# A two-block transformer on one core: first loads split, weights split earlier, retention's heads and PEER's end in another order

## The reference

```
# first block, for l in 0, 1
x = x + 0.5 * swiglu(rms_norm(x, ffn1_norm[l]), gate, up, down)        # 1024 -> 2816 -> 1024
h = rms_norm(x, mix_norm[l]); a, g, q, k, v = split(h @ w_in[l])
x = x + concat([conv_module(a, g), diff_attention(q, k, v)]) @ w_out[l]
x = x + 0.5 * swiglu(rms_norm(x, ffn2_norm[l]), gate, up, down)
# second block, for layer in 0, 1
mod = silu(c) @ ada_w[layer] + ada_b[layer]         # shifts, scales and gates
x = x + g1 * mixer(modulate(rmsnorm(x), sh1, sc1))  # layer 0: retention (4 heads), layer 1: sgu
x = x + g2 * peer_ffn(modulate(rmsnorm(x), sh2, sc2))
# at the end
return rmsnorm(x, norm_final)
```

## Time and profile before

| what | value |
| --- | --- |
| median of three runs | 3076.28 us |
| the three runs | 3084.94, 3076.28, 3075.04 us |
| the profiled execution's own time | 3079.91 us |
| its span in the profile | 3078.1 us |
| PE busy | 3023.9 us, 98% |
| DVE busy | 2184.3 us, 71% |
| ACT busy | 1611.1 us, 52% |
| POOL busy | 266.6 us, 9% |
| from HBM | 616.55 MB |

### The profile page before, as it was taken

One profiled execution on the slowest core, in us unless ns is written; L12 is line 12 of the kernel. 1 busy time (PEld: TensorE's weight loads), 2 busy tenths in 40 slices (PEclk: granted clock), 3 DMA queues, 4 the chain that ended last, 5 costly groups with the idle time before them and its releaser, 6 DMA issues.

```text
span 3078.1 us, 53282 instructions
## 1 busy us (share of the span) xinstructions
PE 3023.9 (98%) x22540; PEld 2851.7 (93%) x22540; DVE 2184.3 (71%) x3454; ACT 1611.1 (52%) x2390; POOL 266.6 (9%) x249
## 2 busy tenths in 40 slices
PE   8999999999999999999999999999999999999999
PEld 8998999999899998999999998879999999999887
DVE  5877887876788746899555557675669975555676
ACT  5575544565544455556544445556445554444444
POOL 0010001000101001830000000000156000000000
PEclk9999999999999999999999999999999999999999
DMA  6772577775267544457866657655444687666663
GB/s 230 268 250 96 205 252 253 266 268 194 97 248 282 179 154 172 157 179 286 290 218 218 215 201 244 210 182 187 165 168 175 233 298 238 218 218 218 220 232 123
DMA packets 153260, 654.59 MB, mean 213 GB/s; under 512 B 10332, under 2 KB 77472, under 8 KB 78272
## 3 DMA queue, kind: packets, MB, share of 16 engines
q1 hardware_dynamic: 96576, 584.09, 53.3%
q10 hardware_dynamic: 56032, 65.66, 6.4%
q0 software_dynamic: 416, 1.45, 0.2%
HBM read 616.55 MB, written 34.61 MB: 212 GB/s over the span
## 4 chain that ended last, share of the span: by engine, by line
PE 88%; DVE 8%; ACT 2%; issue 1%; DMA 1%; POOL 0%; ACTq 0%; DVEq 0%
PE ps L596 19%; PE ps L598 19%; PE ps L597 19%; PE ps L601 8%; PE ps L602 8%; PE ps L603 8%; DVE w_lo L1544 2%; PE ps L1025 2%; PE ps L764 2%; ACT w_hi L1094 1%; DVE raw L1539 0%; DVE h_lo L1562 0%; PE ps L996 0%; DVE at L2034 0%; DVE at L2024 0%
## 5 line engine op out<-in xcount | busy, mean ns | idle before, releaser
L1544 DVE TENSOR_TENSOR w_lo<-raw,w_hi 128x1024 fp32r<-128x1024 f32 x932 | 1137.7, 1227 | 597.8 <-ACT w_hi L1094 596.7
L1094 ACT ACTIVATE w_hi<-raw 128x1024 fp32r<-128x1024 f32 x1000 | 1050.6, 1055 | 679.7 <-PE ps L598 429.2
L596 PE MATMUL ps<-h_hi,w_hi 128*128 128x256 f32 x4224 | 1186.2, 281 | 7.3 <-DVE w_lo L1544 6.1
L597 PE MATMUL ps<-h_lo,w_hi 128*128 128x256 f32 x4224 | 1177.0, 279 | 0.0
L598 PE MATMUL ps<-h_hi,w_lo 128*128 128x256 f32 x4224 | 1176.8, 279 | 0.0
L596 PEld LDWEIGHTS ps<-h_hi,w_hi 128*128 128x128 f32 x4224 | 794.1, 188 | 13.5 <-issue 6.2
L598 PEld LDWEIGHTS ps<-h_hi,w_lo 128*128 128x128 f32 x4224 | 799.9, 189 | 0.0
L597 PEld LDWEIGHTS ps<-h_lo,w_hi 128*128 128x128 f32 x4224 | 795.0, 188 | 2.8 <-issue 0.2
L601 PE MATMUL ps<-w_hi,at 128*128 128x512 f32 x1024 | 398.5, 389 | 3.1 <-DVE at L2083 3.1
L602 PE MATMUL ps<-w_lo,at 128*128 128x512 f32 x1024 | 398.3, 389 | 0.0
L603 PE MATMUL ps<-w_hi,at 128*128 128x512 f32 x1024 | 398.3, 389 | 0.0
(11 more groups left out here) (281 smaller groups left out, 3259.1 us busy)
## 6 DMA issues: line engine op xcount, KB each, us to landing
raw<-in_peer_u SPq DMA_DIRECT2D x128, 1024.0 KB, 4.8
raw<-in_peer_v SPq DMA_DIRECT2D x128, 1024.0 KB, 4.8
raw<-in_ffn_gu SPq DMA_DIRECT2D x88, 1024.0 KB, 4.9
raw<-in_ada_w SPq DMA_DIRECT2D x48, 1024.0 KB, 5.2
raw<-in_ffn_down SPq DMA_DIRECT2D x44, 1024.0 KB, 4.9
gates<-at ACTq DMA_DIRECT2D x32, 1024.0 KB, 4.6
at<-gates ACTq DMA_DIRECT2D x24, 1024.0 KB, 5.9
raw<-in_w_in SPq DMA_DIRECT2D x16, 1024.0 KB, 4.8
```

The source lines that it names most:

```text
L596: e.matmul(o, lhs[0], rhs[0], start=start, stop=False)
L597: e.matmul(o, lhs[0], rhs[1], start=False, stop=False)
L1094: e.activation(whi[:, u % NPAIR, :], raw(k, half), ACT.Copy).then_inc(hi_done.hit(u), 1)
L1544: e.tensor_tensor(wlo[:, m % NPAIR, :], raw(k, half), whi[:, m % NPAIR, :].bitcast(FP), ALU.subtract).then_inc(w_lo_dve.hit(m), 1)
```

## The change

It does the following.

1. **First loads.** x is loaded in two halves (ACT's queue, with the columns of gains between them), the first raw tile in two halves (SP's queue, `raw_first`). The second raw tile waits for x's first half, the third for its second. ACT splits unit 0, then all of h, then unit 1; before it was unit 0, 1, then h. PE no longer waits for `ident`, `half` and x at its start, and its first pair is two `project` calls in turn in place of the interleaved pair. `lam` moves behind the first four splits.
2. **First FFN.** ACT splits units 8 and 9 ahead of `rr`, the silu table and silu of c; before they came among the first silu steps. DVE does the same.
3. **Mixer's output.** Each of ACT and DVE splits one unit more before it waits for x and h there, ACT does its two `h_split` before its two `square`, and `NSUM` of q = 2 and 5 falls from 6 to 4: POOL adds four squares, ACT makes four, and PE sums two of these inside the next FFN's first pair (`inside`).
4. **Adaptive weights.** 17 of each 80 tiles are skipped in place of 14, and the rest stand closer (48 per 122 positions in place of 128).
5. **Retention.** Three banks for scores, gates and sums, four for `attend`. PE does `attend` after pairs 1, 2, 4, 5 and `finish` after 2, 3, 5, 6. DVE inverts a head's root at once and finishes that head a pair later (`invert`, `split`). Nothing stands between pair 7 and `ret_out` on PE. 
6. **PEER's end.** The last pair of `peer_v` runs accumulators 0 and 1 for both units before 2 and 3. ACT copies three accumulators, DVE the last. ACT's squares have five buffers (`square_tile`) for q = 8 and 10.

```diff
-NSUM = {1: 7, 2: 6, 3: 7, 4: 7, 5: 6, 6: 7, 7: 7, 9: 7}
+NSUM = {1: 7, 2: 4, 3: 7, 4: 7, 5: 4, 6: 7, 7: 7, 9: 7}
...
-        seen += not 33 <= i % 80 < 47
-        while n_ada < 48 and n_ada < (seen - 2) * 48 // 128:
+        seen += not 33 <= i % 80 < 50
+        while n_ada < 48 and n_ada < (seen - 2) * 48 // 122:
...
+        ATTEND, FINISH = {1: 0, 2: 1, 4: 2, 5: 3}, {2: 0, 3: 1, 5: 2, 6: 3}
...
+            def project_pairs(q, key, n, outs, lag=2, inside=None):
                 for at in range(KT + lag * (len(outs) - 1)):
+                    if at == inside:
+                        added_sums(q)
+                        sums(q, at, at)
+                        sums(q, at + 1, at + 1)
...
                     if f == 0:
-                        project_pairs(q, (f"{which}_gu", l), 0, [b])
-                        if c > 0:
+                        if c == 0:
+                            for half in range(2):
+                                project(q, unit[(f"{which}_gu", l), half], b[:, half * T:(half + 1) * T])
+                        else:
+                            project_pairs(q, (f"{which}_gu", l), 0, [b], inside=NSUM[q] if NSUM[q] < KT - 2 else None)
+                        if c == 2:
                             added_sums(q)
-                        for m in (0, 1) if c == 0 else range(NSUM[q], KT):
+                        for m in (0, 1) if c == 0 else range(max(NSUM[q], KT - 2), KT):
                             sums(q, m, m)
...
# PE, retention
-                    if n % 2 == 1:
-                        attend(n // 2)
-                    if n % 2 == 0 and n >= 2:
-                        finish(n // 2 - 1)
-                finish(3)
+                    if n in FINISH:
+                        finish(FINISH[n])
+                    if n in ATTEND:
+                        attend(ATTEND[n])
...
# PE, peer
-                    for e2 in range(2):
+                    for e2, ks in ((0, range(4)), (1, range(4))) if n < 63 else ((0, (0, 1)), (1, (0, 1)), (0, (2, 3)), (1, (2, 3))):
...
-                        for k in range(4):
+                        for k in ks:
...
-                        t.then_inc(used.hit(g), 1)
+                        if ks[-1] == 3:
+                            t.then_inc(used.hit(g), 1)
...
# ACT, ffn and mixer
-                token_scale(q, unit[(f"{which}_gu", l), 1] + 1 + NPAIR if c > 0 else 0)
+                ahead = 1 if c > 0 else 5
+                token_scale(q, unit[(f"{which}_gu", l), ahead] + 1 + NPAIR)
...
+                w_hi_upto(unit[("w_out", l), 4] + NPAIR)
                 for n in range(4):
-                    w_hi_upto(unit[("w_out", l), 4 + n] + NPAIR)
+                    if n < 3:
+                        w_hi_upto(unit[("w_out", l), 4 + n] + 1 + NPAIR)
                     w.wait_ge(x_upd, x_upd(q + 1, 2 * n + 1))
                     for m in (2 * n, 2 * n + 1):
                         h_split(q + 1, m, gains)
+                    for m in (2 * n, 2 * n + 1):
                         if m >= NSUM[q + 1]:
                             square(q + 1, m, m)
...
# ACT, peer's end
-                for k in range(2):
+                for k in range(3):
                     w.wait_ge(acc_done, acc_done(l, k))
-                    e.activation(orow[:, k, 0:512], acc[k], ACT.Copy).then_inc(orow_a.hit(l, k), 1)
+                    e.activation(orow[:, k % 2, k // 2 * 512:k // 2 * 512 + 512], acc[k], ACT.Copy).then_inc(orow_a.hit(l, k), 1)
...
# ACT, start
-            e.dma_start(x, a["x"]).then_inc(loads["x"].sem, 16)
+            e.dma_start(x[:, 0:4], a["x"][:, 0:4]).then_inc(loads["x"].sem, 16)
             e.dma_start(cols, a["cols"]).then_inc(loads["cols"].sem, 16)
+            e.dma_start(x[:, 4:8], a["x"][:, 4:8]).then_inc(loads["x2"].sem, 16)
...
-            w_hi_upto(2)
+            w_hi_upto(1)
             w.wait_ge(loads["cols"], 16)
-            w.wait_ge(loads["x"], 16)
             for m in range(KT):
+                w.wait_ge(loads["x" if m < 4 else "x2"], 16)
                 h_split(0, m, col("ffn1_norm", 0))
+            w_hi_upto(2)
...
# DVE, mixer's output
+                w_lo_upto(unit[("w_out", l), 4] + NPAIR)
                 for n in range(4):
-                    if n < 3:
-                        w_lo_upto(unit[("w_out", l), 4 + n] + NPAIR)
                     w.wait_ge(*unit_after(("w_out", l), 4 + n))
...
+                    if n < 3:
+                        w_lo_upto(unit[("w_out", l), 4 + n] + 1 + NPAIR)
                     for m in (2 * n, 2 * n + 1):
                         h_split(q + 1, m, gains)
...
# DVE, retention
-                    if n % 2 == 0 and n >= 2:
-                        finish(n // 2 - 1)
+                    if n in (3, 4, 6):
+                        finish((3, 4, 6).index(n))
+                    if n in FINISH:
+                        invert(FINISH[n])
                 finish(3)
...
# SP, start
-                if 0 < k < NRAW:
-                    w.wait_ge(loads["x"], 16)
+                if k == 0:
+                    e.dma_start(raw_t[:, 0, 0:UNIT], src[:, 0:UNIT]).then_inc(raw_first.sem, 16)
+                    e.dma_start(raw_t[:, 0, UNIT:2 * UNIT], src[:, UNIT:2 * UNIT]).then_inc(landed[0].sem, 16)
+                    continue
+                if k < NRAW:
+                    w.wait_ge(loads["x" if k == 1 else "x2"], 16)
```

More of the change, by code:

```diff
@@ L266, in build @@
         banks = Banks([0, 1, 2, 3, 4, 5])
-        loads = {n: signal(f"load_{n}") for n in ("x", "cols", "ident", "half", "c", "iota", "relb", "oh", "anti")}
+        loads = {n: signal(f"load_{n}") for n in ("x", "x2", "cols", "ident", "half", "c", "iota", "relb", "oh", "anti")}
         consts = signal("consts_set", lambda n: n + 1)
@@ L675, in scale_row @@
                 w.wait_ge(rc_inv, rc_inv(q))
+                w.wait_ge(loads["ident"], 16)
                 for tt in range(2):
@@ L771, in qk_sums @@
                     w.wait_ge(qk_sq, qk_sq(l, i))
+                    w.wait_ge(loads["half"], 16)
                     for tt in range(2):
@@ L895, in retention @@
                     project_rows(q, "ret_v", c, 2 + c, ("rv", c))
+                wide = Banks([banks.ids[(banks.at + d) % 6] for d in (1, 2, 3, 4)])
+                narrow = Banks([banks.ids[(banks.at + d) % 6] for d in (5, 6)] + [6])
                 def scores(hh):
-                    b = take(banks, ("rsc", hh))
+                    b = take(narrow, ("rsc", hh))
                     w.wait_ge(rq_rot, rq_rot(2 * hh + 1))
@@ L909, in attend @@
                     for e2 in range(2):
-                        b = take(banks, ("ratt", hh, e2))
+                        b = take(wide, ("ratt", hh, e2))
                         for z in range(2):
@@ L917, in finish @@
                 def finish(hh):
-                    b = take(banks, ("rfin", hh))
+                    b = take(narrow, ("rfin", hh))
                     for z in range(4):
@@ L924, in retention @@
                 for n in range(8):
-                    b = take(banks, ("rg", n))
+                    b = take(narrow, ("rg", n))
                     project(q, unit["ret_g", 2 * n], b[:, 0:T])
@@ L1068, in _ @@
             w.wait_ge(consts, 1)
-            w.wait_ge(loads["ident"], 16)
-            w.wait_ge(loads["half"], 16)
-            w.wait_ge(loads["x"], 16)
             for l in range(L):
@@ L1506, in _ @@
             e.activation(rcol, epsc, ACT.Sqrt)
+            w_hi_upto(1)
+            w.wait_ge(loads["cols"], 16)
+            for m in range(KT):
+                w.wait_ge(loads["x" if m < 4 else "x2"], 16)
+                h_split(0, m, col("ffn1_norm", 0))
             w_hi_upto(2)
-            w.wait_ge(loads["cols"], 16)
-            w.wait_ge(loads["x"], 16)
-            for m in range(KT):
-                h_split(0, m, col("ffn1_norm", 0))
             for n, m in ((4, 0), (6, 2), (7, 4), (8, 6)):
@@ L1682, in ffn @@
                     if f == 0:
-                        w_lo_upto(unit[(f"{which}_gu", l), 1] + 1 + NPAIR)
+                        w_lo_upto(unit[(f"{which}_gu", l), 1 if c > 0 else 5] + 1 + NPAIR)
                         w.wait_ge(rr_ready, rr_ready(q))
@@ L1846, in finish @@
                     stepped()
+                def finish(hh):
+                    r = rrs[hh % 2]
                     for e2 in range(2):
@@ L2092, in peer @@
                         pair(("peer_u", l), n + NPAIRS)
[L2093 to L2095 removed]
+                w.wait_ge(*unit_after(("peer_v", l), 127))
+                e.tensor_copy(orow[:, 1, 512:1024], acc[3]).then_inc(orow_v.hit(l), 1)
                 for m in range(KT):
```

48 lines of the change are left out of this document (27 added, 21 removed).

## The result

Five runs of the changed kernel took 3062.91 to 3076.46 us with a median of **3065.01 us**; five of the kernel before 3075.04 to 3084.94 with 3076.28. The ratio is 0.9949 with the interval [0.9931, 0.9967]: faster, by 0.5%. The two medians by themselves are 11.3 us apart (0.9963), which lies within that interval. Two later measurements against more runs of the kernel before gave 0.9941 [0.9927, 0.9956] and 0.9951 [0.9937, 0.9966]. The predicted 3068.1 us lies inside the range that was given, but the likeliest case was "same within 0.3%", and that was wrong. The waits of PE gave about the 8.2 us that I had summed. The three ratios say 15 to 18.

What follows compares the result with a forecast made beforehand. PE was taken as the bound, with at most 54 us of idle or lower-clock time to win. Terms summed to -8.2 us, which against the median of 3076.28 gave 3068.1 us, range 3061.5 to 3075.

Steps and rivals of the forecast that it cites:

- Start: Program start: PE begins sooner by reordered loads and splits, -1.5 us, bounds -0.8 and -2.5.
- First FFN: First FFN: PE's waits of 1.59 and 0.51 us for `w_lo` go, -2.1 us, bounds -2.6 and -0.5.
- Mixer's output: Both mixers' outputs: waits for splits go, two added sums cost 0.9 us each time; -2.2 and -0.9 us.
- The gap at 876: PE's gap of 1.11 us at 876.39, following rotary work on DVE: no change, 0, bounds -1.1 and +1.5.
- Retention: Retention's end: 3.40 us of PE idle go except 0.4 us of waiting; -3.0 us, bounds -3.4 and -1.0.
- Start of the first PEER: First PEER's start: a table load of 1.28 us now stands before `rcol`; +1.4 us, bounds 0 and +2.
- the switch costs double: Rival, first PEER's start: ACT pays as much again around a table load, another 1.3 us, giving 3069.4; chance 0.04.
- PEER's ends: PEER's ends: accumulator copies come later in the first, +1.0 us; final sums close up in the second, -0.9 us.
- the clock takes part back: Rival: two stretches at 0.50 clock, at the start and retention's border, grow; gain only 4.8 us, 3071.5; chance 0.17.
- more is won: Rival: half-clock stretches shrink at two places (-3.4 us) and the 1.11 us gap goes; 12.7 us won, 3063.6; chance 0.20.
- Gaps move: Rival: splits are only late at another unit, leaving -1.4 us in all, 3074.9; chance 0.09.
- DVE becomes the bound: Rival, first block's FFNs: closer adaptive tiles make PE wait 1.11 us at 16 places, 3085.9, slower; chance 0.05.

Runs made afterwards that it cites:

- r_after: The changed kernel measured once more with no edit: 3066.38 us, ratio 0.9941 to the kernel before.
- x_noret: The changed kernel with retention's old sequence of heads: 3073.52 us, ratio 0.9962 to the kernel before.
- x_nopeer: The changed kernel with PEER's end as before: 3068.73 us, ratio 0.9958 to the kernel before.
- x_best: The changed kernel with the root's table loaded behind retention's last split, and ACT's and DVE's last split behind the accumulator copies at PEER's end: 3065.75 us, ratio 0.9948.
- x_adaonly: The kernel before with only the adaptive tiles' positions changed: 3077.06 us, ratio 0.9981.
- x_nomix: The changed kernel with the mixer's output as before: 3072.04 us, ratio 0.9969 to the kernel before.
- x_root: The changed kernel with the root's table loaded right behind retention's last split, ahead of ret_out: 3064.95 us, ratio 0.9938 to the kernel before.
- x_mixonly: The kernel before with the mixer's output alone changed, adaptive tiles as before: 3076.69 us, ratio 0.9984.
- x_retonly: The kernel before with retention's new sequence alone: 3081.73 us, ratio 0.9985.
- k_twice: The changed kernel with the scale-spreading matmuls made again at two places in the second FFN (third and fifth pair): 3071.66 us in one execution.

## Why the prediction was wrong

**The bound** was right: PE, and its waits for splits. What I missed is that PE's own rate has two values at the full clock. The sentence "only time in which PE stands idle, or runs at the lower clock, can be won ... 54 us at the very most" leaves out the 33 us that PE lost to the slower rate while it was busy at the full clock. I had read "73 matmuls in 8.20 us (0.112 us each)" and taken it for the rate of the whole kernel. The same view over 345 to 530 us gives 118 ns. It was there to be read in the trace before, and no step of mine compared the rate of one stage with that of another like it.

**The terms by their steps** (first trace of each, with the others where they differ):

- Start, predicted -1.5: PE begins 1.25 sooner (11.92 and 11.78 to 10.67, 10.73 and 10.79). Within the bounds. The first raw half landed at 5.75 us, 2.1 sooner than the whole tile at 7.87, but the first `w_hi` starts at 7.84 for 7.89: ACT's one more load moved its table load by 0.77 and took the place of the wait of 0.73. At the first row of scales 1.0 us is left on average (34.2 us in six traces with the old start, 33.2 in eleven with the new), because the stretch at 0.50 with which the program begins ends anywhere between 13.8 and 17.8 us.
- First FFN, -2.1: the two gaps are gone, 0.41 at 74 us stands for 0.31 before and 0.4 more in small ones; r_after has none. -1.6 to -2.4. Right, but for the wait of 1.1 to 2.0 us where down begins that x_noret, x_nopeer and x_best show.
- Mixer's output, -2.2 and -0.9: -2.64 and -1.24, from row to row of scales. The gaps went as predicted; the two added sums were mis-sized at 0.9. In the second layer 1.76 of waits went for 1.24 of time, so they cost 0.5. For the 1.31 I had named the splits and the tile together; it was the tile alone (x_adaonly, x_nomix).
- The gap at 876, 0: three gaps of 1.66 for 1.11, so +0.55, within the bounds. Two of them (0.65 and 0.52) are waits of over 0.5 us for `w_lo` in an FFN of the first block, which I had named as a sign that the forecast is wrong.
- Retention, -3.0: 3.40 of waits gone, and the 0.4 that I left for DVE's low parts did not appear. From the norm ahead of retention to that of the first PEER, eight traces with the new sequence and the table's load take 209.4 us on average, seven with the old one 211.2: 1.8 less, where 3.4 - 1.4 = 2.0 was to be had.
- Start of the first PEER, +1.4: 2.11 - 0.69 = 1.42, by a load of 1.28 that x_root hid again. Right. The load is followed by `rcol` 0.02 us behind it, so that the rival by which the switch costs double fell.
- PEER's ends, +1.0 and -0.9: +0.4 and -1.1. The copies came 1.36 us later by the cause that I gave, but the sums behind gave back more. That the 1.3 us fitted was luck: I had priced 6 matmuls with the 0.218 of a stretch at half the clock, but these are matmuls of 512 columns, 0.227 each at the full clock. And my floor of 4.1 us for the last sums was too high: they take 3.7.

Together these are about -9 us, so the terms were nearly right as a sum. **Two steps failed.** The first is the sum of -8.2, with the sentence "The terms' own bounds ... give 3065 to 3071.5": it held only waits and added work, and put PE's rate at one value. It lacked the second FFN at 118 ns in place of 113, 6.9 us: 187.90 in the four traces with the stop of 1.31 and no addition, 180.98 or 180.99 in the ten without. The second is the rival "the clock takes part back": I let the stretches at 0.50 only shift, as the one trace had none at the first block's stops. In 5 of 6 traces with the stop of 1.59 one of 3.4 us stands right behind it, and in 4 of 5 with the stops of 1.2, 0.6 and 1.3 (and in x_mixonly, with one of 0.81); in none of the other traces does one stand at either place. Behind the mixer's stops such a stretch costs 1.4 to 1.6 us (129.47, 129.51 and 129.67 us from row to row for 128.03), near the 1.7 that I had. In the first FFN it costs 0.3 to 0.7 in four of five traces, once the slow rate is taken off, because the wait of 0.51 at 50 us is then gone. An estimate from these: 5/6 x 0.8 + 4/5 x 1.5 = 1.9 us more are won by taking the stops out. 9 + 6.9 + 1.9 = 18 us, to be held against the measured 15 to 18. The slow rate in all other stages moves by several us from one execution to the next, so this is no exact account.

A third cause is the base. The median of 3076.28 us came from runs at the low end; in the later sets the kernel before had 3082 to 3086 us. So it is partly luck that 3065.01 us lies near the forecast of 3068.1: the base was low and the gain was larger. The rival "more is won" came nearest by its time (3063.6), though by neither of its reasons alone: the stretches spared are those of the first block, and the gap at 876 did not go. "Gaps move" and "DVE becomes the bound" fell: closer tiles cost the 0.55 us behind the second mixer and little else that was shown.

**Open** stays what retention is worth beyond its waits (1.8 us by its stage; 5 us in x_retonly's total and 3 to 7 in x_noret's, with intervals that reach down to 0), what delays the operand of down in some executions, and why the stretches at 0.50 behind PEER's borders differ in one and the same kernel (ahead of the first PEER 3.4 and 6.8 us in the kernel before, 6.8 and 10.2 in the changed one).

## What to carry to other kernels

Where an engine is busy for 98% of the span, compare its rate in stages of the same shape (count over time) before counting its waits: here a rate that differs by 4% over 188 us outweighed every wait. Price a stop of the bounding engine by what follows it too, the stretch at the lower clock and the rate in which it goes on, and look at several traces of the kernel before, since one need not show them. Here a side job on a border of stages, an adaptive tile at 340 us, cost its own 1.3 us and 6.9 more.

## What the runs showed of the hardware

TensorE did float32r matmuls of 128x256 every 113 ns or every 118 ns at granted clock 1.00, in even episodes of up to 190 us in an FFN. A group of four matmuls of 128x128 turned one rate into the other in 104 of 106 cases, and two groups turned it and turned it back (k_twice, one execution). Eight to twelve matmuls of 128x1 with no wait behind them left the rate at 118 ns in 99 of 99 cases. The stop of 1.59 us in the first FFN was followed by 3.4 us at half the clock in 5 of 6 traces, and the stops at the first mixer's output (1.2, 0.6 and 1.3) in 4 of 5. But the stops of 1.8 and 1.4 to 1.6 us at retention's end were followed by none in any of 7 traces, nor those of 1.2 and 0.6 at the second mixer's output in 7. So the length of a stop alone did not tell whether the clock would fall.
